# Output stage of a two-layer backbone on one core: cheaper norms, a smaller share of routing, another order

## The reference, cut to what matters

```
  h = LN(alpha * h + gate1 * concat(A,B,C,D) @ W_out) * g + b     (DeepNorm post-norm)
  h = LN(alpha * h + gate2 * PEER(LN(h) * (1 + scale2) + shift2)) * g + b

  q = (tb @ w_q).reshape(PEER_BLOCK, 8 heads, 2, 128)
  s = einsum('thpd,hpnd->thpn', q, keys)              # 128 keys for each half of a head
  top_s, top_i = lax.top_k(s, 16)
  cand = top_s[:, :, 0, :, None] + top_s[:, :, 1, None, :]       # 256 candidates
  best_s, pos = lax.top_k(cand, 16)                   # -> expert numbers and gates
```

## Time and profile before

| what | us |
|---|---|
| median of 3 runs (5439.28 to 5479.49) | 5472.81 |
| the profiled execution's own time | 5459.72 |
| its span | 5457.9 |
| PE busy | 4469.8 |
| DVE busy | 3612.6 |
| ACT busy | 1890.8 |
| POOL busy | 1849.0 |

### The profile page before, as it was taken

How to read it: one execution, slowest core, us unless ns; L and a number is a source line. 1 busy time by engine, 2 the same in 40 slices (tenths; PEclk the granted TensorE clock), 3 DMA queues, 4 the chain that set the end, 5 groups by cost and what they waited for, 6 DMA issues and landing times. The chain is left out here.

```text
span 5457.9 us, 77338 instructions
## 1 busy us (share of the span) xinstructions
PE 4469.8 (82%) x27814; PEld 2438.9 (45%) x27814; DVE 3612.6 (66%) x7825; ACT 1890.8 (35%) x5409; POOL 1849.0 (34%) x1903
## 2 busy tenths in 40 slices
PE   7997788779797887978788887697886979788777
PEld 3454578435252342524333344366863525243222
DVE  1675577677768676676765547656767776767644
ACT  2333422124343434334344323342212334343333
POOL 0240033035444444444443313203303544444432
PEclk9997999899999999999999998768988999999999
DMA  7776443379999999999999967404437999999998
GB/s 266 235 223 237 174 133 116 140 296 414 421 421 421 419 416 419 413 420 415 397 421 422 393 216 229 130 19 120 126 127 296 414 421 421 421 420 418 420 421 349
DMA packets 420562, 1719.25 MB, mean 315 GB/s; under 512 B 98152, under 2 KB 202136, under 8 KB 252568
## 3 DMA queue, kind: packets, MB, share of 16 engines
q0 software_dynamic: 200832, 1387.51, 62.6%
q1 hardware_dynamic: 197896, 299.39, 15.9%
q10 hardware_dynamic: 21456, 27.40, 1.5%
HBM read 1624.93 MB, written 92.94 MB: 315 GB/s over the span
## 5 line engine op out<-in xcount | busy, mean ns | idle before, releaser
L2697 PE MATMUL pe_ps<-pe_ring,lent 128*128 128x512 f32 x5120 | 2448.4, 613 | 580.1 <-ACT lent L2782 573.4
L2264 POOL DMA_INDIRECT pe_ring<-in_peer_uv,ro_slot x1280 | 1445.4, 1129 | 2172.9 <-PE pe_ps L2697 1760.5
L2857 DVE SCALAR_TENSOR_TENSOR pe_ring<-pe_ring,ro_tb 128x1024 f32<-128x1024 f32 x1280 | 1561.5, 1226 | 935.1 <-DMA pe_ring<-in_peer_uv,ro_slot 916.3
L2697 PEld LDWEIGHTS pe_ps<-pe_ring,lent 128*128 128x128 f32 x5120 | 900.0, 191 | 1973.9 <-ACT lent L2782 1247.4
L2776 ACT ACTIVATE pe_wts<-pe_raw 128x1 f32<-128x1 f32 x1280 | 258.2, 202 | 1679.6 <-DVE pe_ring L2857 1678.0
L2782 ACT ACTIVATE lent<-c_ident,pe_wts 128x128 f32<-128x128 f32 x1280 | 513.9, 402 | 41.9
L2778 ACT ACTIVATE pe_wts<-pe_wts,ro_gates 128x1 f32<-128x1 f32 x1280 | 376.5, 294 | 41.6
L1039 PE MATMUL pp_ps<-pp_opening 128*128 128x439 f32 (+2 forms) x864 | 313.8, 522 | 11.8 <-issue 10.5
L1570 POOL TENSOR_TENSOR ch_m<-ch_at,ch_joins 128x256 f32<-128x256 f32 x288 | 206.8, 754 | 320.0 <-DVE ch_at L1857 320.0
L2321 PEld LDWEIGHTS pe_ps<-ro_tbT,peer_wq 128*128 128x128 f32 x2048 | 248.8, 192 | 61.2 <-issue 61.2
L1039 PE MATMUL pp_ps<-peer_wq 128*128 128x384 f32 (+5 forms) x704 | 235.6, 496 | 36.5 <-issue 15.2
(11 more groups left out here) (407 smaller groups left out, 5197.8 us busy)
## 6 DMA issues: line engine op xcount, KB each, us to landing
at_aw<-in_w_ada SPq DMA_DIRECT2D x10, 4096.0 KB, 13.7
pe_ring<-in_peer_uv,ro_slot POOLq DMA_INDIRECT x1280, 15.0
peer_wq<-in_peer_wq SPq DMA_DIRECT2D x16, 1024.0 KB, 7.7
pp_opening<-in_w_in SPq DMA_DIRECT2D x9, 1756.0 KB, 8.8
lent<-gdt_dram SPq DMA_DIRECT2D x22, 640.0 KB, 8.1
gdt_dram<-pp_turn_gout POOLq DMA_DIRECT2D x40, 320.0 KB, 8.2
peer_wq<-in_w_in SPq DMA_DIRECT2D x7, 1756.0 KB, 11.4
rwt_dram<-pp_turn_out POOLq DMA_DIRECT2D x48, 256.0 KB, 5.0
```

What stands on the lines that cost most here:

```text
L2264: return pool.indirect_dma_start(dst, None, table, bass.IndirectOffsetOnAxis(ap=index, axis=0))
L2697: mm = pe.matmul(ps[:, y_bank(p) + c, :], diag[:, n % DIAGS, :], ring[:, n % RING, D + c * 512:D + (c + 1) * 512], start=(k == 0), stop=(k ...
L2857: v.scalar_tensor_tensor(row, row, 1.0, tb[p % 2][:], ALU.mult, ALU.mult, accum_out=raw[p % 2][:, k:k + 1]).then_inc(dots_done, 1)
```

## The change

It touches the output stage and the first tile's steps of the gather stage.

1. **Norms.** The residual pass also sums its result; `sum_to_mean` makes minus the mean; ScalarE squares the deviation with an accumulator (into the tile's own PSUM banks, or for the route norm into the scores' buffer) and takes the root with bias and scale; two VectorE passes do subtract, scale and the affine parts. This goes for all tiles' norms in the output stage and the first tile's route norm, not for those of the gather stage.
2. **Routing.** Two heads here (`PARTS[0]`, 15 steps), then two (`PARTS[1]`, steps 8 to 22) and four (`PARTS[2]`, steps 23 to 51) beside the first gathers. One group of queries here, three there (12 queries in steps 1 to 16, scores at 6, 12, 18). The next tile's turn moves from step 16 to 26. POOL waits before rows 32 and 64.
3. **Weights.** Two of W_out's eight k-tiles (1 MB) are loaded in the chunk stage, into what is later the first place of the ring.
4. **Order.** On VectorE tile 2's post work comes ahead of tile 0's norm, and each tile's square on ScalarE is given other VectorE work beside it, but for tile 0 and the route norm. On TensorE tile 2 is turned ahead of the route's turn, tile 3 between queries and scores. On ScalarE tile 2's root stands ahead of tile 1's copies, and a tile's `z_deviation` takes the place of its root. On SP tile 2's inputs move ahead of the affine rows, and the gate's load is a step of its own.

```diff
+def sum_to_mean(v, mv, mean_ready):
+    v.tensor_scalar(mv[:, 1:2], mv[:, 0:1], -1.0 / D, None, ALU.mult).then_inc(mean_ready, 1)
+def squared_deviation(act, spare, x, mv, squared):
+    act.activation(spare, x, ACT.Square, bias=mv[:, 1:2], accum_out=mv[:, 2:3]).then_inc(squared, 1)
+def deviation(act, mv, consts, std_ready):
+    act.activation(mv[:, 3:4], mv[:, 2:3], ACT.Sqrt, bias=consts["layer"][:, 3:4], scale=1.0 / D).then_inc(std_ready, 1)
+def ln_scaled(v, link, out, x, by, mv):
+    link(v.reciprocal(mv[:, 4:5], mv[:, 3:4]))
+    link(v.scalar_tensor_tensor(out, x, mv[:, 1:2], by, ALU.add, ALU.mult))
 ...
+                    elif c == KT:
+                        sp.dma_start(w_first, t["w_out"][l].rearrange("(k p) n -> p k n", p=P)[:, 0:2]).then_inc(w_first_in, 16)
 ...
-                load_w(0)
+                load_w(1)
                 load_y(1)
-                for k in range(1, 4):
+                for k in range(2, 4):
                     load_w(k)
                 load_h(0)
+                load_gate(0)
+                load_y(2)
                 for dst, src in ((g[:], over_rows(t["ln_mix_g"][l])), (bb[:], over_rows(t["ln_mix_b"][l]))):
 ...
                 turn_y(0)
                 mix(0)
                 turn_y(1)
                 mix(1)
+                turn_y(2)
                 route_turn(pe, r, 0)
-                pe.wait_ge(keys_in, 64)
-                for q in range(2):
-                    route_queries(pe, r, 0, q)
-                for q in range(2):
-                    route_scores(pe, r, 0, q)
-                turn_y(2)
-                for j in range(2, NT):
+                pe.wait_ge(keys_in, 32)
+                route_queries(pe, r, 0, 0)
+                turn_y(3)
+                route_scores(pe, r, 0, 0)
+                mix(2)
+                for j in range(3, NT):
 ...
+                def z_deviation(j):
+                    act.wait_ge(z_mean, j + 1)
+                    squared_deviation(act, mixed(j), z[j % 2][:], mv[j % 2], mix_free)
+                    act.wait_ge(mix_free, j + 1)
+                    deviation(act, mv[j % 2], consts, z_std)
 ...
                 turned_y(0)
                 po_roots(1)
+                po_roots(2)
                 turned_y(1)
-                z_root(0)
-                route_root(act, r, 0)
+                z_deviation(0)
+                row_deviation()
+                turned_y(2)
                 for n in range(2):
                     route_turned(act, r, 0, n)
-                po_roots(2)
-                z_root(1)
-                for q in range(2):
-                    route_keep_queries(act, r, 0, q)
-                for q in range(2):
-                    route_keep_scores(act, r, 0, q)
                 po_roots(3)
-                turned_y(2)
+                z_deviation(1)
+                route_keep_queries(act, r, 0, 0)
                 turned_y(3)
                 if NT > 4:
                     po_roots(4)
+                route_keep_scores(act, r, 0, 0)
 ...
                     link(v.tensor_tensor(mixed(j), mixed(j), gate[:], ALU.mult))
-                    v.scalar_tensor_tensor(x[:], x[:], ALPHA, mixed(j), ALU.mult, ALU.add).then_inc(mix_free, 1)
-                    v.wait_ge(mix_free, j + 1)
-                    ln_first(v, link, x, stats, mv, z_var)
+                    link(v.scalar_tensor_tensor(x[:], x[:], ALPHA, mixed(j), ALU.mult, ALU.add, accum_out=mv[j % 2][:, 0:1]))
+                    sum_to_mean(v, mv[j % 2], z_mean)
 ...
-                po_first(1)
-                po_last(1)
+                po(1)
+                po(2)
                 post_first(0)
                 post_last(0)
-                v.wait_ge(z_ready, 1)
-                route_norm_first(v, link, r, 0)
-                route_norm_last(v, link, r, 0)
-                po_first(2)
-                po_last(2)
+                route_norm()
+                po(3)
                 post_first(1)
-                post_last(1)
-                po_first(3)
-                po_last(3)
-                route_steps(0, 8)
                 if NT > 4:
+                    po(4)
+                    post_last(1)
+                    route_steps(0, 4)
                     post_first(2)
+                    po(5)
+                    post_last(2)
+                    route_steps(4, 8)
+                    post_first(3)
+                    route_steps(8, 13)
+                    post_last(3)
+                    post_first(4)
+                    route_steps(13, 14)
+                    post_last(4)
+                    post_first(5)
                     route_steps(14, 15)
+                    post_last(5)
+                else:
+                    route_steps(0, 4)
+                    post_last(1)
+                    route_steps(4, 8)
+                    post_first(2)
+                    route_steps(8, 11)
                     post_last(2)
+                    route_steps(11, 14)
+                    post_first(3)
                     route_steps(14, 15)
+                    post_last(3)
 ...
-HALF_QUERY_AT = [1 + j for j in range(8)]
-HALF_SCORE_AT = [6, 10]
-HALF_AT = {8 + 8 * n // 5: n for n in range(HALF_STEPS)}
-HALF_EXPS_AT = 8 + 8 * 13 // 5 + 1
+PARTS = (slice(0, 2), slice(2, 4), slice(4, 8))
+PART_QUERY_AT = [1, 2, 3, 4, 6, 7, 9, 10, 12, 13, 15, 16]
+PART_SCORE_AT = [6, 12, 18]
+PART_AT = ({8 + n: n for n in range(15)}, {23 + 7 * n // 5: n for n in range(21)})
+PART_EXPS_AT = (16, 42)
+FIRST_TURN_AT = 26
 ...
-                    if n == SLOTS // 2:
-                        pool.wait_ge(half_slot, 1)
+                    for part in range(1, len(PARTS)):
+                        if n == PARTS[part].start * TOPK:
+                            pool.wait_ge(half_slot, part)
```

More of the change, by code:

```diff
@@ L2544, in ahead_steps, with peer_stage @@
     return places
-def peer_stage(nc, l, t, s, b, wq, lent, consts, out):
+def peer_stage(nc, l, t, s, b, wq, place, lent, consts, out):
     tiles = mix_tiles(l)
@@ L2602, in _ @@
                     k = n % SLOTS
[L2603 removed]
+                    gather_row(pool, t["peer_uv"], ring_row(n), slot[n // SLOTS % 3][:, k:k + 1]).then_inc(row_in[n % RING], 16)
                 pool.wait_ge(pe_used, N)
@@ L2840, in _ @@
                         if at - 1 in SCORE_AT:
-                            if p == 0 and at - 1 == SCORE_AT[0]:
-                                act.wait_ge(half_slot, 1)
+                            for part in range(1, len(PARTS)):
+                                if p == 0 and SCORE_AT.index(at - 1) == PARTS[part].start // 2:
+                                    act.wait_ge(half_slot, part)
                             route_keep_scores(act, r, p + 1, SCORE_AT.index(at - 1))
@@ L2854, in dot @@
                     p, k = n // SLOTS, n % SLOTS
-                    row = ring[:, n % RING, 0:D]
+                    row = ring_row(n)[:, 0:D]
                     row_here(v, n)
@@ L2906, in _ @@
                             route_step(v, link, r, p + 1, SEARCH_AT[late(p, k)])
-                    if p == 0 and k in HALF_AT:
-                        route_half_step(v, link, r, 1, HALF_AT[k], half_slot)
+                    for part in range(1, len(PARTS)):
+                        if p == 0 and k in PART_AT[part - 1]:
+                            kept_before = (PARTS[part].start - PARTS[1].start) // 2
+                            route_part_step(v, link, r, PARTS[part], PART_AT[part - 1][k], lambda g: (half_s_kept, kept_before + g + 1), half_slot, part)
                 for part in range(6):
```

236 lines of the change are left out of this document (125 added, 111 removed).

## The result

The changed kernel takes 5407.7 us (median of 20 runs, 5393.9 to 5461.2), the one before 5447.2 (median of 20 runs, the three of the prediction among them). The ratio is 0.9936, 95% interval 0.9917 to 0.9956: 35 us faster, between 24 and 45, and within 1%. The forecast was 45 us less, of 5472.8. The before it started from was 26 us too high, so it says 5428 where its difference, taken from 5447, gives 5402. That difference of 45 lies at the edge of what was measured.

What follows compares the result with a forecast made beforehand. VectorE's list was taken to bound the output stage, and transfers the gathers. Output stages -55 (-28 and -27) and gathers +10 gave -45, so 5472.8 became 5428 us, range 5400 to 5462.

Steps and rivals of the forecast that it cites:

- Layer 0, -28: Layer 0's output stage: ends at 1104.0 against 1132.3, TensorE the bound, 7 us of VectorE's saving idle.
- Layer 1, -27: Layer 1's output stage: VectorE bounds, 34.2 us from the scores' keep to 1074.9; the old end is 1101.8.
- The Square: Output stage norms: ScalarE's square of 1024 elements takes 1.1 us, 1.45 with root and handovers.
- rival C: Output stage norms: Square needs another table than Sqrt, two loads, 2.6 us, in each wait; -25 us, 5448; chance 0.10.
- three exposures a layer: Output stage: the Square's wait counts three times a layer; at 0.55 or 2.4 us, 2 more or 8 less.
- The gathers, +5 a layer: First gathers, steps 8 to 51: VectorE has 120.9 us of work against 109.1; loss 5 us a layer, between 0 and 9.
- the slack of 7: First gathers: the ring and first loads take up 7 us of VectorE's 11.8 too much, between 2.7 and 13.
- the dip around steps 45 to 51: First gathers: DMA's rate falls under 420 GB/s around these steps, some 5 us a layer.
- Rivals B: First gathers: first loads and the ring swallow all 11.8 us; -55, 5418 or a little under; chance 0.21.
- D (22 a layer): First gathers: VectorE's 11.8 and TensorE's 10 us fall one after the other; -11 in all, 5462; chance 0.15.
- I cost them at nothing: Chunk stage: loading two k-tiles of weights there costs nothing, 0 to 1 us if DMA's cover is gone.
- Rival E: Output stage: TensorE's granted clock falls to half and stays, products take 82 us more; +37, 5510; chance 0.03.

Runs made afterwards that it cites:

- Experiment 5: Changed kernel with each Square of the output stage done twice on ScalarE: output stages 124.5 and 96.2 us, +6.9 and +6.7.
- experiment 1: Kernel before with only its norms changed, old order, routing split and loads kept: ratio 0.998 to the kernel before, output stages -0.7 and -3.0 us.
- experiments 8 and 9: On the changed kernel: 8 moved the next tile's norm to steps 22 and 24, ratio 0.9925; 9 also moved its searches to steps 53 to 79, ratio 0.9899.
- experiment 3: Changed kernel with the old split of the routing, four heads in the output stage and four beside the gathers: ratio 0.9954 to the kernel before.
- experiment 7: Changed kernel with next tile's norm at steps 22 and 24, searches at 53 to 79, and early W_out load moved to the fourth chunk: ratio 0.9916.
- experiment 10: Changed kernel with next tile's norm at steps 22 and 24, searches at 53 to 79, and tile 2's post work behind the route norm: ratio 0.9906.

## Why the prediction was right, and where it was not

**Layer 0, -28: right, one step hidden.** In the coordinates of before, tile 2's inputs were waited for 3.3 us (2.7 forecast), the second product started at 1013.0 (1013.1), mix(2) at 1040.7 (after scores at 1040), the last product ended at 1097.6 (1097), the stage at 1104.8 (1104.0). TensorE is the bound and 6.4 us of VectorE's saving go idle (7). What the sum did not need was off: behind a gap of 4.24 us (the prediction had the new ones "under 3") the granted clock was 0.71 from 1016.59 to 1022.00, the first eight matmuls of the second product took 5.26 us instead of 3.60, and it ended at 1028.6, not 1026.9. The queries started that much later, and ScalarE's square ahead of their copy hid it: that TensorE was late here cost nothing is luck.

**Layer 1, -27: right in mechanism, 1.7 us off.** From the scores' keep VectorE took 35.0 us (34.2), and the scores were kept 1.1 us later than I said.

**The Square and rival C.** 1.12 to 1.15 us (1.1), a wait of 1.64 (1.45), a norm of 7.1 us exposed (6.95), a route norm of 4.5 (4.45), two table loads. C is out. Square needs no load behind Sqrt, and none behind Exp either: the one at 1081.39 ran with Exp's tables loaded, and the load came only with the root at 1082.65. The rule that cheap functions are filler in every set (Trainium skill, ScalarE: Activation LUTs, Table sets: the hidden batching unit) does not name Square; this trace bears it out for Square. The switch that it gives as about 2.7 us (the page counts a drain in) took 1.28 here each time, with the next instruction right behind it.

**What I did not see about the norms.** The prediction charged the Square as a wait of VectorE, three exposures a layer, and in layer 0 as what the queries' copy stands behind. Experiment 5 shows a little over five, and experiment 1 shows a further way: the bank is released by ScalarE, later than VectorE had released it. In the changed order that costs little, and so the sum was not hurt. As a statement on what the norms are worth by themselves it would have been wrong by 12.6 us (16.3 expected, 3.7 measured).

**The gathers, +5 a layer: about right in sum, wrong in place, and with too large a slack.** They lost 6.1 and 7.6, inside the 0 to 9. That the sum of VectorE's work over the stretch sets the loss is borne out by experiments 8 and 9: with the sum unchanged 1.9 and 0.7 came back, with 7.4 us of searches taken out as well 6.5 and 6.7 did. The term that was mis-sized is the slack of 7. By the prediction's own count, overloads of 11.8 and 4.4 us cost 6.4 to 7.3 and nothing clear of the scatter in the first tiles against before, so the slack was 5 or so. Against experiment 3, the same kernel with the old split, they cost 9 and 2.4 (first tiles 338.1 and 337.9, 331.6 and 331.2, over 329.2 and 328.8), and it was 2 to 3. The two differ because experiment 3's gathers are 3.0 and 1.6 us shorter than before's, for a reason that no run isolates. So part of the 5 is luck: what the moved routing took back is 9 a layer. POOL's two new waits held nothing, as forecast: the slots for row 64 were written 149.1 us behind the first dot, and its gather went out at 169.7. VectorE was busy for 111.1 of the 119.2 us up to dot 51, 93% and not "over 95%". I looked for the dip around steps 45 to 51 only; nearly half of the lost transfer time is already spent at steps 15 to 26, where the norm falls among route steps that come with every row. Rivals B (nothing) and D (22 a layer) are out.

**The step that failed: "I cost them at nothing, because that stage moves far less than DMA carries (0 to 1 us if that cover is gone)".** Two k-tiles of weights in the chunk stage cost that stage 6 us in layer 1, in nine profiles against three, and perhaps 4 in layer 0, though it carried only 134 GB/s up to the last chunk's turn and 93 behind it. The mean rate was a bad guide to a stage that is a chain of small loads, stores and products. By what way the load costs 6 us is open: some 2 go with its place (experiment 7), 1.2 do not. The whole time can't settle the term: -39.2 for the four stretches is inside the measured -24 to -45 without it, and -29 is with it. Undone on its own the load gave no gain, as the output stage then paid 3.3 and 3.8 us.

**Rival E** didn't come: behind the dip at the second product layer 0's clock was full from 1022.00 on, and the last product ran from 1087.24 to 1101.14, 13.90 us, the warm time of the earlier trace rows.

**Where the gain is from**, by undoing one thing at a time: the split of the routing 13.5 us net, the norms 13.5, the early load 7.1 in the output stages (which the chunk stages pay back), tile 2's place 0 and -2.5. Such parts need not add up. If they do, some 8 of the 39.2 are the remaining order, which I did not take apart further; the post work of tile 4 ahead of the searches, for which TensorE idled 10.85 us in the earlier trace rows, is a likely part, not a shown one.

## What to carry to other kernels

Work that was moved under a stage bound by transfers was free only up to the ring's slack, and what counted was its sum over the stretch up to the deadline, not how dense it stood. So first see what in that stretch has no deadline and push that out: here that was worth as much as the norms. When a pass moves to another engine, ask what its last instruction used to release. And cut two profiles into stages before you believe their difference, and see whether the cut itself moved: 1.1 us of a "cost" here was a landmark that came earlier.

## What the runs showed of the hardware

The attention stage of layer 1 has the same instructions in all thirteen profiles, and took 180 us in eight, 201 in three and 224 in two. The clock granted to TensorE falls from full to half in the middle of it, and the length goes by when: 120, 84 and 50 us into the stage in those of 180, 201 and 224 us. Before (201.7 us), the changed kernel (180.2) and experiment 10 (224.0), in windows of 30 us each:

```profile
3561.90:3591.90 30.00, 26.22 (x166) 18.32 (x165) 23.62 (x38) 16.00 (x35) 0.00 (x0) 1.00 0.12 40
3591.90:3621.90 30.00, 27.91 (x122) 19.17 (x122) 17.06 (x28) 11.01 (x26) 0.00 (x0) 0.66 0.01 5
3621.90:3651.90 30.00, 28.66 (x102) 19.70 (x101) 10.79 (x18) 9.01 (x20) 0.00 (x0) 0.50 0.00 1
```

```profile
3568.30:3598.30 30.00, 26.55 (x173) 18.72 (x171) 21.89 (x37) 16.56 (x38) 0.00 (x0) 1.00 0.02 5
3598.30:3628.30 30.00, 25.05 (x119) 17.15 (x118) 19.17 (x31) 10.53 (x23) 0.00 (x0) 0.76 0.01 5
```

```profile
3501.80:3531.80 30.00, 26.80 (x171) 18.86 (x172) 20.95 (x33) 15.00 (x35) 0.00 (x0) 1.00 0.10 36
3531.80:3561.80 30.00, 28.21 (x103) 18.32 (x102) 15.94 (x27) 9.37 (x22) 0.00 (x0) 0.57 0.01 5
```

At full clock 30 us hold some 170 matmuls, at half (1.2 GHz) some 100, with TensorE busy 25 to 29 of 30 either way; it had been busy at the full clock up to the fall. Why it falls at a different place in different executions stays open. This alone makes 20 to 44 us of a profile's total, as much as the whole change.

A VectorE pass over 128x1024 with two tensors and a scalar from memory took 1.28 us, without it 1.22. The read of ScalarE's accumulator took 0.19 us, that of VectorE's 0.08.
